# One-core Trainium2 kernel of two stacked mixer blocks: squares of norms added on VectorE, norm rows off GpSimd, filter taps in row halves, filter transforms in four PSUM banks

## What is computed

```python
def rms_norm(x, g, eps=NORM_EPS):
    y = xf * lax.rsqrt(jnp.mean(xf * xf, axis=-1, keepdims=True) + eps)
    return (y * g)
hx = rms_norm(x, norm_pre[l]) * (1.0 + sc_x) + sh_x      # input of a layer
x  = x + rms_norm(ux @ w_out[l], norm_post[l]) * gt_x    # output of a layer
```

## Time and profile before

| | us |
|---|---|
| three timed runs | 2635.17, 2641.04, 2640.37 (median 2640.37) |
| profiled execution, device time | 2635.36 |
| profiled execution, span | 2633.6 |
| TensorE busy in the span | 2535.8 (96%) |
| VectorE, ScalarE, GpSimd busy | 1090.9, 766.1, 408.3 |
| mean granted TensorE clock | 0.989 |

### The profile page before, as it was taken

The page is one execution under the profiler, slowest core; times in us unless marked ns, Lnnn a source line. Parts: engine busy times, 40 slices in busy tenths (PEclk is TensorE's granted clock), DMA queues, the critical chain, the costliest instruction groups (busy, mean ns, idle before and its releaser), DMA issues.

```text
span 2633.6 us, 63024 instructions
## 1 busy us (share of the span) xinstructions
PE 2535.8 (96%) x27894; PEld 1682.7 (64%) x27894; DVE 1090.9 (41%) x2254; ACT 766.1 (29%) x1531; POOL 408.3 (16%) x439
## 2 busy tenths in 40 slices
PE   5999999999999997999999999999999999999998
PEld 1466666666666666668887754446444468775786
DVE  3765566666555663343652231105511113322412
ACT  2444444444454442131221210014300013102301
POOL 2433333334433340000010000000000000000000
PEclk8999999999999997999999999999999999999999
DMA  6211111111111113724336522220233343331342
GB/s 238 94 37 45 37 51 40 37 37 47 37 45 37 49 27 129 279 72 152 128 137 248 199 96 72 72 80 5 94 122 120 116 160 127 126 115 60 98 150 92
DMA packets 82053, 257.34 MB, mean 98 GB/s; under 512 B 11607, under 2 KB 19384, under 8 KB 81080
## 3 DMA queue, kind: packets, MB, share of 16 engines
q1 hardware_dynamic: 75176, 241.89, 27.0%
q10 hardware_dynamic: 6000, 8.28, 0.9%
q0 software_dynamic: 608, 3.15, 0.3%
HBM read 252.23 MB, written 1.05 MB: 96 GB/s over the span
## 4 chain that ended last, share of the span: by engine, by line
PE 57%; DVE 1%; ACT 1%; ACTq 1%; DMA 0%; issue 0%; SPq 0%; DVEq 0%
PE ps L1873 14%; PE ps L2042 9%; PE ps L1817 8%; PE ps L1753 6%; PE ps L2059 5%; PE ps L1907 4%; PE ps L1947 1%; PE ps L1698 1%; PE ps L1987 1%; PE ps L1967 1%; PE ps L1932 1%; PE ps L1774 1%; PE ps L1927 1%; PE ps L1762 1%; PE ps L1794 1%; ACTq L2367 1%
## 5 line engine op out<-in xcount | busy, mean ns | idle before, releaser
L1873 PE MATMUL ps<-h,ring 128*128 128x256 f32 (+1 forms) x1184 | 363.5, 465 | 0.0
L1873 PEld LDWEIGHTS ps<-h,ring 128*128 128x128 f32 x1184 | 225.0, 190 | 126.2 <-issue 107.1
L2042 PE MATMUL ps<-h,ring 128*128 128x512 f32 (+1 forms) x768 | 256.1, 486 | 0.0
L1817 PE MATMUL ps<-h,ring 128*128 128x256 f32 x1024 | 225.2, 379 | 0.8 <-ACT general L2205 0.8
L1817 PEld LDWEIGHTS ps<-h,ring 128*128 128x128 f32 x1024 | 193.9, 190 | 34.5 <-issue 7.7
L2042 PEld LDWEIGHTS ps<-h,ring 128*128 128x128 f32 x768 | 145.2, 190 | 103.1 <-issue 93.2
L1014 ACT ACTIVATE general<-general 64x512 f32<-64x512 f32 x160 | 101.8, 636 | 156.7 <-DVE general L1213 154.1
L556 PE MATMUL ps<-general,ring 128*128 128x512 f32 x256 | 134.9, 623 | 0.8 <-issue 0.8
L572 PE MATMUL ps<-general,ring 128*128 128x512 f32 x256 | 134.2, 629 | 0.0
L2953 POOL TENSOR_TENSOR h<-h,rstd 128x256 f32<-128x256 f32 x15 | 13.0, 882 | 762.4 <-ACT rstd L2176 762.4
L2059 PE MATMUL ps<-general,ring 128*128 128x512 f32 (+1 forms) x384 | 131.0, 486 | 0.0
(11 more groups left out here) (358 smaller groups left out, 4086.3 us busy)
## 6 DMA issues: line engine op xcount, KB each, us to landing
ring<-in_w_mods SPq DMA_DIRECT2D x96, 512.0 KB, 5.4
ring<-in_w_feature SPq DMA_DIRECT2D x74, 512.0 KB, 3.2
ring<-in_w_rkvg SPq DMA_DIRECT2D x64, 512.0 KB, 3.6
ring<-in_w_in SPq DMA_DIRECT2D x48, 512.0 KB, 3.2
ring<-in_w_merge SPq DMA_DIRECT2D x48, 512.0 KB, 3.5
ring<-in_w_out SPq DMA_DIRECT2D x32, 512.0 KB, 5.9
ring<-in_w_token SPq DMA_DIRECT2D x24, 512.0 KB, 3.8
ring<-in_w_merge SPq DMA_DIRECT2D x48, 256.0 KB, 2.9
```

The lines of the kernel that those rows point to most:

```text
L1817: mm = pe.matmul(ps[:, n % 4, 0:NX], weights(key, k), R.h[:, k, 0:NX], start=(k == 0), stop=(k == KD - 1))
L1873: mm = pe.matmul(ps[:, j % 4, 0:width], weights(("feature", l, j), k), R.h[:, k, cols], start=(k == 0), stop=(k == KD - 1))
L2042: mm = pe.matmul(ps[:, 2 * b, 0:NQ], weights(key, k), R.h[:, k, 0:NQ], start=(k == 0), stop=(k == KD - 1))
```

## The change

Five edits, all after the scan.

1. **Squares added on VectorE.** VectorE adds rows 1 to 6 of the squares into row 0 (`out_added`, `state_added`, each waiting for the square and for the add before it), and a norm has two products, of row 0 and of row 7. The output passes call `out_added(p, m - 1)` after `out_copy(p, m)`; in pass 0 it is `out_added(0, m)` after the filter steps of row m.
2. **Norm rows on VectorE alone.** `added` takes all 8 rows, in order; GpSimd has none. In pass 3 it is split in two halves behind `out_copy(3, 0)` and `out_copy(3, 1)`, and the eight `state_square(3, k)` are split likewise. `out_sum(2)` moves behind the first row of pass 3.
3. **Filter layers and `w4` doubled** onto partitions 64 to 127 (the layers as two products side by side in column groups, loads of `f_vec` and `w4` with 128 partitions, so 1 MB more). Sum and difference are two operations in place of three, and nothing is copied.
4. **Taps in row halves.** The sum's tap comes from partitions 0 to 63, the difference's from 64 to 127, in a pair, into banks 3 and 7; a pair waits until both of the last were taken out.
5. **Transforms in four banks** (3, 7, 6, 2). ScalarE copies 12 out, VectorE four (3, 7, 11, 15). The wait for all copies moves from before the first Hyena tile to before the third. `state_sum(0)` stands after 8 transforms, not 9.

```diff
+FILTER_FIRST, FILTER_LAST = (1, 2, 0, 4, 0, 5, 0, 6), (8, 9, 10, 0, 12, 0, 13, 14)
+FILTER_BANKS = (3, 7, 6, 2)
-    def out_sum(p, m):                       # one product a row, eight a norm
+    def out_sum(p):
+        if p:
+            pe.wait_ge(s["o_log"], p)
+        pe.wait_ge(s["o_acc"], 6 * (p + 1))
+        pe.matmul(ps[:, 4, 0:NX], R.ones[:, :], sq(0), start=True, stop=False)
+        pe.wait_ge(s["o_sq"], 8 * p + 8)
+        pe.matmul(ps[:, 4, 0:NX], R.ones[:, :], sq(7), start=False, stop=True).then_inc(s["o_sum"], 1)
...
-        for n in range(16):
-            t, q, ch = n // 8, n // 4 % 2, n % 4
-            if n >= 2:
-                pe.wait_ge(s["f_out"], n - 1)
-            pe.matmul(ps[:, bank[n % 2], :], W.hid[0:64, t:NX:2], W.w4[0:64, q, ch * 512:(ch + 1) * 512],
+        for n in range(8):
+            t, ch = n // 4, n % 4
+            if n:
+                pe.wait_ge(s["f_out"], 2 * n)
+            for q in range(2):
+                r = slice(64 * q, 64 * q + 64)
+                mm = pe.matmul(ps[:, (3, 7)[q], :], W.hid[r, t:NX:2], W.w4[r, 0, ch * 512:(ch + 1) * 512], start=True, stop=True)
...
-    pe.wait_ge(s["s_act"], 16)
     for n, key in enumerate(order):
+        if n == 2:
+            pe.wait_ge(s["s_act"], 12)
+            pe.wait_ge(s["s_dve"], 4)
         hyena_tile(n, key)
...
+    filter_out(0)
     for k in range(KD):
         state_square(0, k)
-        filter_out(k)
-    filter_out(KD)
+        if FILTER_FIRST[k]:
+            filter_out(FILTER_FIRST[k])
...
+    def out_added(p, m):
+        t, side = PASSES[p]
+        acc, new = (W.squares[t][:, n, HALF[side]] for n in (0, m))
+        dve.wait_ge(s["o_sq"], 8 * p + m + 1)
+        if m > 1:
+            dve.wait_ge(s["o_acc"], 6 * p + m - 1)
+        dve.tensor_tensor(acc, acc, new, ALU.add).then_inc(s["o_acc"], 1)
...
         for _ in range(FILTER_ITEMS[m]):
             next(filt)
+        if 0 < m < KD - 1:
+            out_added(0, m)
     in_gain(0)
-    added(0)
+    added(0, 0, 5)
+    filter_out(3)
+    added(0, 5, KD)
+    for k in range(1, KD - 1):
+        state_added(0, k)
+    filter_out(7)
     for k in range(KD):
         scaled(0, k)
+    filter_out(11)
+    filter_out(15)
...
         added(p)
+        for k in range(1, KD - 1):
+            state_added(q, k)
         for j in range(GAP_FIRST):
             feature(l, j)
```

More of the change, by code:

```diff
@@ L2090, in finish_pe @@
             modulation_turn(1, m // 6)
-        if m:
-            out_sum(0, m - 1)
         for _ in range(FILTER_ITEMS[m]):
             next(filt)
-    out_sum(0, KD - 1)
-    for _ in range(9):
+    out_sum(0)
+    for _ in range(8):
         next(filt)
-    for k in range(KD):
-        state_sum(0, k)
+    state_sum(0)
     for _ in filt:
@@ L2131, in finish_pe @@
             feature(l, j, j == 0)
-        for k in range(KD):
-            state_sum(2 + 2 * l, k)
+        state_sum(2 + 2 * l)
         for j in range(GAP_FIRST, GAP):
@@ L2151, in finish_pe @@
                     modulation_turn(3, 1)
-                if m:
-                    out_sum(p, m - 1)
+                if p == 3 and m == 0:
+                    out_sum(2)
                 if p == 3 and m == 3:
-                    for k in range(KD):
-                        state_sum(3, k)
-            out_sum(p, KD - 1)
+                    state_sum(3)
+            if p != 2:
+                out_sum(p)
 def finish_act(act, R, W, I, S, s, layer):
@@ L2441, in finish_act @@
                 out_square(p, m)
-                if p == 3 and m == 0:
-                    for k in range(KD):
+                if p == 3 and m < 2:
+                    for k in range(4 * m, 4 * m + 4):
                         state_square(3, k)
@@ L2523, in filters @@
             dve.wait_ge(s["f_layer"], n + 1)
-            a, r = W.arg[0:64, :], W.rnd[0:64, :]
-            step(dve.tensor_scalar(a, ps[0:64, 3, 0:NX], fb[0:64, n:n + 1], fb[0:64, 3:4], ALU.add, ALU.mult))
+            a, r = W.arg, W.rnd
+            step(dve.tensor_scalar(a, ps[:, 3, 0:NX], fb[:, n:n + 1], fb[:, 3:4], ALU.add, ALU.mult))
             step.wait()
@@ L2876, in finish_dve @@
         out_copy(1, m, ("out1", m, 1))
+        for k in (2 * m, 2 * m + 1):
+            if 0 < k < KD - 1:
+                state_added(1, k)
         if m in (2, 6):
             mods_out(2, m // 6)
+        if m > 1:
+            out_added(1, m - 1)
         if m == 5:
@@ L2918, in finish_dve @@
                 out_copy(2, m, ("last", 0, C_HALF, m))
+                if m > 1:
+                    out_added(2, m - 1)
                 if m == 0:
@@ L2922, in finish_dve @@
                 out_copy(3, m, ("last", 0, X_HALF, m))
+                if m < 2:
+                    added(2, 4 * m, 4 * m + 4)
                 if m == 0:
-                    added(2)
                     out_gain(3)
+                if m > 1:
+                    out_added(3, m - 1)
+                if m == 2:
+                    for k in range(1, KD - 1):
+                        state_added(3, k)
                 if m == 4:
@@ L2933, in finish_dve @@
                 out_copy(4, m, ("last", 1, X_HALF, m))
+                if m > 1:
+                    out_added(4, m - 1)
             added(4)
 def finish_pool(pool, R, W, I, S, s, layer):
[L2939 to L2956 removed]
     def distances(l):
@@ L3077, in layouts @@
     out["f_w23"] = np.stack([a["l1_f_w2"], a["l1_f_w3"]], 1)
-    out["f_vec"] = np.stack([a["l1_f_b1"], a["l1_f_b2"], a["l1_f_b3"], a["l1_sin_freq"]], 1)
-    out["f_w4"] = a["l1_f_w4"].reshape(64, 2, E)
+    out["f_vec"] = np.tile(np.stack([a["l1_f_b1"], a["l1_f_b2"], a["l1_f_b3"], a["l1_sin_freq"]], 1), (2, 1))
+    out["f_w4"] = np.tile(a["l1_f_w4"].reshape(64, 2, E), (2, 1, 1))
     out.update(hyena_constants())
```

160 lines of the change are left out of this document (69 added, 91 removed).

## The result

| | before | after |
|---|---|---|
| median of the timed runs | 2638.43 us (4 runs, 2635.17 to 2641.04) | 2608.16 us (4 runs, 2605.72 to 2610.98) |
| ratio, 95% interval | | 0.9881 [0.9868, 0.9894] |
| profiled execution, device time; span | 2635.36; 2633.6 | 2609.7; 2607.7 |

What follows compares the result with a forecast made beforehand. The prediction took TensorE to bound the kernel. Its terms summed to 30.8 us saved, giving 2604.6 from the profiled 2635.36, or 2609.6 since the median of runs was 5.0 higher; it took 2607, range 2599 to 2617.

Steps and rivals of the forecast that it cites:

- What bounds it: Whole kernel: TensorE, busy for 2535.8 of 2633.6 us, bounds it; each product removed saves its full length.
- Passes 2 and 3, norms 2 and 4, pass 4's products: Passes 2 and 3 with input norm 3 save 8.8 us, input norms 2 and 4 2.6 each, pass 4's products 2.2.
- The tail: Behind pass 4's last product: 16 norm operations on VectorE alone take 5.4 us in place of 6.6, gain 1.2.
- Pass 1: Six loop products of 0.5 us save 3.0, input norm 1 saves 2.9, the end costs 0.4: gain 5.5 us.
- Exp to the first tile: From the end of pass 0's root Exp to the first Hyena tile: 16.8 us in place of 23.0, gain 6.1.
- Pass 0: Pass 0 to its root: 1.8 us earlier, though the turn behind row 2 comes at 1070.2 in place of 1068.17.
- The clock rival: Clock falls at pass 0's turn, perhaps before input norm 0's products: 2 to 4 us, total 2610; chance 0.25.
- Row halves in turn: Pass 0's tap products on row halves run one after another, 8 x 0.7 us, total 2612; chance 0.05.
- Late adds: VectorE's adds take 0.94 us each, costing about 3 at norm 0, 2 at norms 2 and 4: 2617; chance 0.05.
- The DMA as the bound: The weights' DMA bounds passes 0 and 1, losing their gains of 1.8 and 5.5 us: 2614; chance 0.1.
- Slower, by a clock that stays low: Clock falls at the turn and stays low for the rest of pass 0: +56 us, total 2663; chance 0.02.
- The extra 1 MB ... nothing: The doubled weights load some 55 us before use, under the end of the scan, and cost nothing.

Runs made afterwards that it cites:

- e_pool: The changed kernel with rows 2, 5 and 7 of every norm back on GpSimd: 2613.82 us, ratio 0.9903 to the kernel before.
- e_early: The changed kernel with each add of squares in passes 1 to 4 called one row sooner: 2609.13 us, ratio 0.9896 to the kernel before.
- e_loads: The kernel before with only the loads of f_vec and w4 doubled, the second half read by nobody: 2640.41 us, ratio 1.0012 to the kernel before.
- e_taps64: The changed kernel with filter layers, filter steps, taps and their loads on 64 partitions as before: 2612.05 us, ratio 0.9895 to the kernel before.
- e_late: e_comb with the upper 64 partitions of w4 loaded behind the eight ring loads: 2609.32 us, ratio 0.9894 to the kernel before.
- e_sums: The changed kernel without VectorE's adds, eight products with the ones a norm in a block: 2625.30 us, ratio 0.9942 to the kernel before.
- after2: The changed kernel as it is, timed and profiled a second time: 2607.56 us, ratio 0.9888 to the kernel before.
- e_fill: The changed kernel with 11 transforms in place of 8 ahead of input norm 0's products: 2610.29 us, ratio 0.9900 to the kernel before.
- e_turn: The changed kernel with pass 0's add of rows 0 and 1 behind row 2's filter steps: 2606.22 us, ratio 0.9889 to the kernel before.
- e_actq: The changed kernel with ScalarE's loads of idft and hyena_vec issued behind norm 0's root: 2606.81 us, ratio 0.9888 to the kernel before.
- e_banks: The changed kernel with the filter transforms in two banks, 3 and 7, in place of four: 2607.90 us, ratio 0.9884 to the kernel before.
- e_comb: The changed kernel with e_turn, e_fill and e_early together, in pass 3 earlier adds only from row 3: 2604.91 us, ratio 0.9881 to the kernel before.

## Why the prediction held, and where it was off

The forecast (2607, all squares' products worth their full length) is the case that came, 1.2 us beside the median. So close is partly luck: by the stages the sum was 1.9 too high, 3.2 us of falling clock stood in no term, and the tail and an earlier turn gave back most of it. A granted clock under 1.00 between 1060 and 1150 us was also one of the signs of being wrong that the prediction names. By its steps:

- **What bounds it.** Right: 29.2 us less of TensorE's work, 28.9 us less from pass 0's start to the end.
- **Passes 2 and 3, norms 2 and 4, pass 4's products.** 8.8, 2.4, 2.6 and 2.2, against 8.8, 2.6, 2.6 and 2.2. Here TensorE had no cause to wait beside those counted, so that the count of products was the whole sum. VectorE's six adds at input norms 3 and 4 take 3.06 us together, 0.51 each, near the 0.45 assumed.
- **The tail** gave 2.2 for 1.2. Behind the last product it is 11.06 before and 8.87 after, and again 11.06 in `e_pool`. The rows' own work shrank as counted, from 6.6 to 5.5 us behind the root. The term left out the stores, which SyncE issues in the order of the rows, before and after:

```profile
2629.83 1.79 SPq L1713 DMA_DIRECT2D out_x<-x  x4
```

```profile
2604.30 1.48 SPq L1711 DMA_DIRECT2D out_x<-x  x3
```

Before, four stores stand one behind another at some 0.45 us each, and the last is issued 1.0 us behind VectorE's last operation (2630.14); after, it is issued as that ends (2605.28), and that is the other 1.0 us.
- **Pass 1** gave 4.1 for 5.5. The prediction took 0.5 for a product between modulation steps. But a dense row that is followed directly by a modulation step takes about 0.1 longer than one followed by a product, so that each of the six removed gave 0.42, and the six of input norm 1 gave 2.6 for 2.9. The rest, 0.7, is the wait for the ring of weights behind row 0, 1.94 us after and 1.23 before:

```profile
1421.46 1.89 PE L1698 MATMUL ps<-ring,cond 128*4 128x512 f32 x12 [1.23 <-DMA ring<-in_w_mods]
```

```profile
1418.56 1.89 PE L1699 MATMUL ps<-ring,cond 128*4 128x512 f32 x12 [1.94 <-DMA ring<-in_w_mods]
```

- **Exp to the first tile** gave 4.3 for 6.1. The count was right but for one thing: TensorE idled 2.71 us for the adds (2.3 were predicted), and behind that the clock fell. `e_early`, where it did not fall, has 17.0 us; the prediction had 16.8.
- **Pass 0** gave 2.15 for 1.8, through two errors that cancel. The turn was forecast at 29.6 us after pass 0's start (1070.2 less 1040.60) and came at 27.7, because ScalarE's issue lasted 11.49 us and not the 13.39 of the earlier trace rows. In its place the clock fell, which was the rival of a chance of 0.25. The idle ahead of it was 1.97 us, not the 4.3 worked out.
- **The clock rival** came true in its mechanism, in both places it named, at about its price. Around input norm 0's products the fall costs 1.6 us (18.63 against 17.0). At the turn, L1699 takes 3.00 in place of 1.89 and L1791 1.12 in place of 0.65, 1.6 together. That the total still met the forecast is due to the tail and to the timed runs: the stages alone say 28.9, and the forecast's sum was 30.8.
- **The other rivals.** Row halves in turn: no, a pair of taps is 1.14 with its drain. Late adds: they were not slow (0.51 each) but late: the sums waited for them 2.7 us at input norm 0, 0.9 at the ends of passes 1, 3 and 4, and 0.5 at input norm 3. The DMA as the bound: no; it is wanted more (297 GB/s in place of 280 in pass 1), and its one wait in pass 1 grew by 0.7 us. Slower, by a clock that stays low: no, behind the turn it was back within 4 us.
- **"The extra 1 MB ... nothing"** is neither shown nor refuted. For a cost: `e_loads`, 3 us slower with an interval that leaves out zero, and the kernel before with the earliest start of all profiles (1040.60). Against: `e_taps64` without the 1 MB started at 1045.72, `e_late` with half of it late at 1046.16, and one with all of it at 1041.12. The starts of pass 0 spread from 1040.60 to 1046.77 us over kernels that have the same program up to there but for these loads, so one profile of each can't say what the loads cost, and the spread goes into every timed run. Part of it is the clock, which is low in the scan's end for a time that differs between executions (L789 at 1.98 or 3.68 us, above). What the loads themselves cost, and why `e_loads` was slower in its timed runs, stays open.

What the edits bring, each undone by itself, by the totals from pass 0's start and, in brackets, read without what the clock and the ring's wait did elsewhere: the adds 16.2 us (14.2), the rows off GpSimd 5.2 (7.0), the row halves 0.1 (0.95), the four banks nothing (1.4 in their own stretch). These are 21.5 of 28.9 us by the totals and 23.6 by the brackets. The rest was not tried by itself; `e_sums` still differs from the kernel before in that the sums of a pass stand in a block and not singly between rows, and in the new order of passes 2 and 3.

## What to carry to other kernels

Count what leaves the bounding engine, but at each place where the helper's work ends last, look at what stands ahead of it in its queue, its DMA issues too: an issue that costs 0.35 us with the DMA engines free held ScalarE for 10 to 13 us when they were full and two loads of 1 MB were under way in its own queue. Moving a sum's products behind three more pieces of independent work, and its first add behind the copies that TensorE waits for, was worth 4.4 us of pass 0 and the stretch behind it, for no instruction more, where the clock had fallen behind these waits, and 0.8 where it had not. Where timing can't tell a few us, compare profiles stretch by stretch: here the start of pass 0 moved by 6 us, most stretches repeated within 0.1, and three moved by 1.7 to 2.6 us on the same code, mostly because a wait of some 2 to 3 us did or did not cost the clock.

## What the runs showed of the hardware

**A fall of the clock is not set by the length of the idle alone.** The granted clock behind the idle at the turn and before input norm 0's products, in the kernels' profiles:

| kernel | idle at the turn, us | clock behind it | idle before the products | clock behind it |
|---|---|---|---|---|
| after | 1.97 | fell | 2.71 | fell |
| after2 | 1.89 | fell | 2.71 | fell |
| e_taps64 | 1.90 | 1.00 | 3.31 | fell |
| e_pool | 2.32 | 1.00 | 2.74 | fell |
| e_fill | 2.54 | fell | none | 1.00 |
| e_early | 0.69 | 1.00 | 2.71 | 1.00 |
| e_turn | 0.36 | 1.00 | 2.71 | fell |
| e_actq | 0.69 | 1.00 | 2.71 | fell |
| e_banks | 0.96 | 1.00 | 2.02 | fell |
| e_sums | 0.36 | 1.00 | none | 1.00 |
| e_comb | 0.35 | 1.00 | none | 1.00 |
| e_late | 2.39, for the Sin | fell | none | 1.00 |

An idle of 1.90 and one of 2.32 left 2.4 GHz alone, one of 1.89 did not; 2.71 us cost the clock in four of five profiles. In pass 1 the wait for the ring cost it at 2.04 us (`e_actq`) and 2.35 (`e_sums`), and at 1.15 to 1.94 in no profile. The kernel before is open to it too: an idle of 2.00 among its transforms left the clock at 1.00 in its profile, and the same idle in the same code of `e_loads` brought it to 0.56, which made the stretch from Exp to tile 24.64 us in place of 22.94. The forecast had counted against a fall that 4.3 us is less than the 5.00 of the earlier trace rows. The Trainium skill, "TensorE: Matmul & The Clock Gate", "HAM oscillation", says that idle gaps between bursts of products send the array back to half clock. The table agrees in that every fall stands behind a gap; it adds that one and the same gap brings a fall in one execution and none in another.

**A DMA issue can hold its engine for over 10 us.** The load of 256 KB by L2367 took ScalarE from 10.12 (`e_loads`) to 13.39 us to issue in pass 0 (DMA share 1.04), and 0.35 us behind the root, where the share was 0. It landed 21.6 us after its issue in pass 0, and 2.5 us after it behind the root. Full DMA engines alone don't make an issue long: in the changed kernel SyncE issued a load of 512 KB in 0.33 us at the same share:

```profile
1059.79 0.33 SPq L104 DMA_DIRECT2D ring<-in_w_mods  x1
```

What ScalarE's queue had besides was two loads of 1 MB under way, issued just ahead (they landed 18.4 and 24.6 us after their issue). `e_actq` takes the issue away from both, so which of the two holds it, or whether it takes both, was not tried.

**VectorE beside GpSimd.** With both inputs in SBUF, an operation of VectorE on 256 columns takes 0.42 us alone and 0.94 beside one of GpSimd, in `e_pool` as before the change. The Trainium skill, "GPSIMD Engine Reference", "Specifications", says that the two share their interfaces to SBUF and that VectorE's instructions with two inputs there meet contention; these rows agree.
